# Latent input turned behind every second grouped tile, and a group norm made token tile by token tile

## What is computed

```python
def spatial_gating(z, v_norm, w_s, b_s):          # layer 0
    z = jax.nn.gelu(z)                            # z: (1, 1024, 512)
    u, vv = jnp.split(z, 2, axis=-1)
    u = u.reshape(b, s, B_GROUPS, B_GROUP_DIM)    # 4 groups of 64 columns
    vv = rmsnorm(vv.reshape(b, s, B_GROUPS, B_GROUP_DIM), v_norm)
    vv = vv.reshape(b, s // B_CHUNK, B_CHUNK, B_GROUPS, B_GROUP_DIM)   # chunks of 128 tokens
    mixed = jnp.einsum('gpq,bnqgc->bnpgc', w_s, vv) + b_s.T[None, None, :, :, None]
    return (u * mixed.reshape(b, s, B_GROUPS, B_GROUP_DIM)).reshape(b, s, B_WIDTH)

def mixer_odd(h, ...):                            # layer 1
    proj = h @ w_in
    ...
    cq = (rmsnorm(cq, cq_norm) @ w_cq_up).reshape(b, s, C_HEADS, C_NOPE + C_ROPE)
    kv = (rmsnorm(ckv, ckv_norm) @ w_ckv_up).reshape(b, s, C_HEADS, C_NOPE + C_V)
    ...
    dq = axial_rope(rmsnorm(dq.reshape(b, s, D_KV_HEADS, D_GROUP, HEAD_DIM), dq_norm), row, col)
    dk = axial_rope(rmsnorm(dk.reshape(b, s, D_KV_HEADS, HEAD_DIM), dk_norm), row, col)
    ...
```

## Time and profile before

| | |
|---|---|
| median of 3 runs | 4104.06 us (4103.8 to 4111.27) |
| profiled execution | 4103.9 us, span 4101.7 us |
| TensorE busy | 3662.3 us, 89% |
| VectorE busy | 2458.3 us, 60% |
| ScalarE busy | 1639.6 us, 40% |
| GpSimd busy | 329.3 us, 8% |
| mean granted clock of TensorE | 0.947 |

### The profile page before, as it was taken

How to read it: one execution, slowest core, us unless ns; L and a number is a source line. 1 busy time by engine, 2 the same in 40 slices (tenths; PEclk the granted TensorE clock), 3 DMA queues, 4 the chain that set the end, 5 groups by cost and what they waited for, 6 DMA issues and landing times. The chain is left out here.

```text
span 4101.7 us, 58119 instructions
## 1 busy us (share of the span) xinstructions
PE 3662.3 (89%) x23128; PEld 3009.7 (73%) x23128; DVE 2458.3 (60%) x3918; ACT 1639.6 (40%) x2308; POOL 329.3 (8%) x195
## 2 busy tenths in 40 slices
PE   6988999988999999999799999499788999994996
PEld 4767777877777888887599777377687877773774
DVE  3366671568765556566332663777664776637786
ACT  5223432158320000002221763367534766623775
POOL 0011111000000000000000000133200000001432
PEclk9989999999999999999899999799899999997998
DMA  5011223631431111112221324399723022043998
GB/s 196 16 50 37 75 75 121 240 117 36 157 136 74 55 41 60 42 41 82 93 86 57 132 86 154 143 372 371 268 86 121 28 88 81 23 149 125 371 366 295
DMA packets 194719, 527.57 MB, mean 129 GB/s; under 512 B 27512, under 2 KB 127656, under 8 KB 175424
## 3 DMA queue, kind: packets, MB, share of 16 engines
q1 hardware_dynamic: 178176, 467.21, 31.0%
q0 software_dynamic: 13200, 55.17, 4.6%
q10 hardware_dynamic: 3120, 2.10, 0.2%
HBM read 433.05 MB, written 91.37 MB: 128 GB/s over the span
## 5 line engine op out<-in xcount | busy, mean ns | idle before, releaser
L2556 ACT ACTIVATE mlp_relu<-mlp_z 128x512 f32<-128x512 f32 x64 | 38.3, 598 | 616.2 <-PE mlp_z L168 616.2
L3740 DVE TENSOR_TENSOR ring_r<-ring,oN_r 128x4096 fp32r<-128x4096 f32 x48 | 212.4, 4426 | 72.2 <-ACT oN_r L3646 72.2
L166 PE MATMUL scans_G<-ring_r 128*128 128x512 f32 x544 | 221.8, 408 | 32.3 <-ACT scans_stg L3106 18.3
L3740 DVE TENSOR_TENSOR ring_r<-ring,hT_r 128x4096 fp32r<-128x4096 f32 x48 | 212.5, 4427 | 51.3 <-ACT hT_r L3646 51.2
L3646 ACT ACTIVATE oN_r<-ring 128x4096 fp32r<-128x4096 f32 x48 | 174.0, 3629 | 81.0 <-DMA ring<-in_w_all 79.3
L166 PE MATMUL mlp_z<-oN_r,mlp_w_high_r 128*128 128x512 f32 x512 | 200.3, 391 | 5.6 <-DVE ring_r L2597 5.6
L167 PE MATMUL mlp_z<-hT_r,mlp_w_high_r 128*128 128x512 f32 x512 | 200.0, 391 | 0.0
L168 PE MATMUL mlp_z<-oN_r,ring_r 128*128 128x512 f32 x512 | 199.9, 390 | 0.0
L166 PE MATMUL mlp_y_ps<-mlp_w_high_r,ring_r 128*128 128x512 f32 x512 | 199.7, 390 | 0.0
L167 PE MATMUL mlp_y_ps<-ring_r 128*128 128x512 f32 x512 | 199.2, 389 | 0.0
L168 PE MATMUL mlp_y_ps<-mlp_w_high_r,ring_r 128*128 128x512 f32 x512 | 199.2, 389 | 0.0
(11 more groups left out here) (693 smaller groups left out, 10003.1 us busy)
## 6 DMA issues: line engine op xcount, KB each, us to landing
ring<-in_w_all SPq DMA_DIRECT2D x110, 2048.0 KB, 10.6
ring<-in_w_mlp SPq DMA_DIRECT2D x16, 2048.0 KB, 8.3
ring<-in_w_all SPq DMA_DIRECT2D x12, 1024.0 KB, 6.2
branch_gates<-scans_stg SPq DMA_DIRECT2D x48, 256.0 KB, 2.0
merge_raw<-branch_gates SPq DMA_DIRECT2D x16, 768.0 KB, 5.0
ring<-in_w_all POOLq DMA_DIRECT2D x8, 1024.0 KB, 6.0
diff_gemm_more<-in_w_all POOLq DMA_DIRECT2D x8, 1024.0 KB, 6.2
oN<-x_rows SPq DMA_DIRECT2D x16, 512.0 KB, 7.5
```

The costliest lines, as they stand in the source:

```text
L166: pe.matmul(out, lh, rh, start=start, stop=False)
L2556: act.activation(r[:, n % 2, :], Z[:, n % 4, :], ACT.Relu).then_inc(z_free, 1)
L3740: dve.tensor_tensor(buf_r[:, b, :], buf[:, b, :], w_high[n % RING].bitcast(F32), ALU.subtract)\
```

## The change

Two separate edits. In `odd_gemm_stage` the three latent groups are turned behind tiles 4, 6 and 8 instead of 4, 5 and 6, copied by ScalarE in the same turns, and their low parts are made in turns 5, 7 and 9 instead of 5, 6 and 7. In `spatial_stage` VectorE makes the squares, the sums and the product with the gain for each token tile as soon as its gelu is there; mean, root and reciprocal stay in one piece behind the last tile; the product with the reciprocal root is made group by group (four instructions of 128 x 512 instead of one of 128 x 2048), each of which lets TensorE start one group's mix.

```diff
--- before.py
+++ after.py
@@ -862,8 +862,8 @@
                     tile(NT + n, 1 + s_, t).then_inc(done, 1)
                 if n == 4:
                     pe.wait_ge(low_ready, NT)
-                if 4 <= n < 7:
-                    j = n - 4
+                if n in (4, 6, 8):
+                    j = (n - 4) // 2
                     if j:
                         pe.wait_ge(ct_used, j)
                     for t in range(NT):
@@ -947,9 +947,10 @@
                     act.activation(sq6, A[:, (NT + n) % 4, 0:NB * P], ACT.Square).then_inc(sq_in, 1)
                     act.wait_ge(root_in, n + 1)
                     act.activation(ss[:, n % 2, :], ss[:, n % 2, :], ACT.Sqrt).then_inc(root, 1)
-                if 4 <= n < 7:
-                    act.wait_ge(ct_done, n - 3)
-                    act.activation(c_high[:, n - 4, :], CT[:, :, :].rearrange("p a n -> p (a n)"), ACT.Copy).then_inc(ct_in, 1)
+                if n in (4, 6, 8):
+                    j = (n - 4) // 2
+                    act.wait_ge(ct_done, j + 1)
+                    act.activation(c_high[:, j, :], CT[:, :, :].rearrange("p a n -> p (a n)"), ACT.Copy).then_inc(ct_in, 1)
                 if n >= 1:
                     i = n - 1
                     act.wait_ge(xt_done, i + 1)
@@ -1066,10 +1067,11 @@
                 t5, v5 = (u.rearrange("p g (a b c) -> p g a b c", a=2, b=2) for u in (turned, v))
                 dve.tensor_tensor(t5[:, :, :, 0, :], t5[:, :, :, 0, :], v5[:, :, :, 1, :], ALU.subtract)
                 step(dve.tensor_tensor(t5[:, :, :, 1, :], t5[:, :, :, 1, :], v5[:, :, :, 0, :], ALU.add))
-                if 4 < n <= 7:
-                    dve.wait_ge(ct_in, n - 4)
-                    dve.tensor_tensor(c_low[:, n - 5, :], CT[:, :, :].rearrange("p a n -> p (a n)"),
-                                      c_high[:, n - 5, :].bitcast(F32), ALU.subtract).then_inc(ct_used, 1)
+                if n in (5, 7, 9):
+                    j = (n - 5) // 2
+                    dve.wait_ge(ct_in, j + 1)
+                    dve.tensor_tensor(c_low[:, j, :], CT[:, :, :].rearrange("p a n -> p (a n)"),
+                                      c_high[:, j, :].bitcast(F32), ALU.subtract).then_inc(ct_used, 1)
                 dve.wait_ge(root, n + 1)
                 step(dve.reciprocal(s2, s2))
                 dve.tensor_tensor(v, turned, s2.unsqueeze(2).to_broadcast([P, HEADS, 64]), ALU.mult).then_inc(x_ready, 1)
@@ -2713,8 +2715,8 @@
                     ins = three_passes(pe, Z[:, t % 4, :], [h[:, k, t * P:(t + 1) * P] for h in (h_high, h_low)],
                                        [v[:, k, :] for v in w], k == 0, k == KD - 1)
                 ins.then_inc(z_done, 1)
-            pe.wait_ge(v_ready, 1)
             for g in range(G):
+                pe.wait_ge(v_ready, g + 1)
                 if g >= 2:
                     pe.wait_ge(gated, g - 1)
                 v = z[:, :, W2 + g * C:W2 + (g + 1) * C]
@@ -2741,15 +2743,17 @@
                 dve.tensor_tensor(quarter(buf_r[:, slot, :], j), quarter(buf[:, slot, :], j),
                                   quarter(w_high, j).bitcast(F32), ALU.subtract).then_inc(w_split, 1)
             dve.wait_ge(par_in, 48)
-            dve.wait_ge(z_free, NT)
             v = z[:, :, W2:2 * W2].rearrange("p t (g c) -> p t g c", c=C)
-            group_squares(step, dve, v, sq[:, :, :].rearrange("p t (g c) -> p t g c", c=C), ss[:, :, :])
+            for t in range(NT):
+                dve.wait_ge(z_free, t + 1)
+                group_squares(step, dve, v[:, t, :, :], sq[:, t, :].rearrange("p (g c) -> p g c", c=C), ss[:, t, :])
+                dve.tensor_tensor(z[:, t, W2:2 * W2], z[:, t, W2:2 * W2], gn[:, :], ALU.mult)
             dve.tensor_scalar(ss[:, :, :], ss[:, :, :], 1.0 / C, EPS, ALU.mult, ALU.add).then_inc(root_in, 1)
             dve.wait_ge(root, 1)
             step(dve.reciprocal(ss[:, :, :], ss[:, :, :]))
-            step(dve.tensor_tensor(v, v, ss[:, :, :].unsqueeze(3).to_broadcast([P, NT, G, C]), ALU.mult))
-            dve.tensor_tensor(z[:, :, W2:2 * W2], z[:, :, W2:2 * W2],
-                              gn[:, :].unsqueeze(1).to_broadcast([P, NT, W2]), ALU.mult).then_inc(v_ready, 1)
+            for g in range(G):
+                dve.tensor_tensor(v[:, :, g, :], v[:, :, g, :], ss[:, :, g:g + 1].to_broadcast([P, NT, C]), ALU.mult)\
+                   .then_inc(v_ready, 1)
             for g in range(G):
                 dve.wait_ge(mixed, g + 1)
                 u = z[:, :, g * C:(g + 1) * C]
```

## The result

| | before | after |
|---|---|---|
| median | 4104.02 us (4098.1 to 4113.18, 6 runs) | 4085.55 us (4080.83 to 4088.72, 6 runs) |
| ratio to before | 1 | 0.995, 95% interval 0.9936 to 0.9963 |
| profiled execution | 4103.9 us, span 4101.7 | 4088.72 us, span 4086.6 |

The change makes the kernel 18.5 us faster by the medians, 15 to 26 us by the interval.

The account below looks back on a forecast made before the run. It took TensorE, busy for 89% of the span, to bound the kernel, with time won only where it stands still or runs at its lower clock. 13.2 + 7.7 = 20.9 us less gave 4083.0 us, range 4078.5 to 4091.

Parts of the forecast that it names:

- The thin margin: Grouped loop: TensorE reaches the second and third latent group about 0.5 us after VectorE's low part releases the PSUM tile.
- The 0.2 us in turn 10: Grouped loop: turn 10's transposes come late behind VectorE's turn with a low part, losing about 0.1 to 0.2 us.
- The split of the latent weights: Grouped loop, turn 10: nothing piles up ahead of this split; cost taken as nothing, bounds 0 and 1.22 us.
- a whole turn of VectorE behind a tile of TensorE: Grouped loop before the change: the claimed cost of a latent group, with TensorE idle 4.56 and 4.57 us.
- the clock's: Spatial stage's four mixes: the clock may rise one mix sooner, a gain of 0.4 us, bounds 0 to 0.9.
- The 0.5 us by which the first gating might have been late: Spatial stage: VectorE's first gating, queued behind the fourth product, ends up some 0.5 us past the first mix at worst.
- the loop's term: Grouped loop: 13.38 us less over four turns, less 0.2, gives a gain of 13.2 us, bounds 11 and 13.6.
- the spatial term: Spatial stage: first mix 7.3 us earlier plus 0.4 us of clock, a gain of 7.7 us, bounds 5.5 and 8.2.
- Rival 2: Grouped loop: the 0.5 us margin is used up by late turns, 2 us a group, 4087.0 us in all; chance 0.10.
- rival 3: Spatial gain hidden because the next stage waits for something other than the barrier; 13.2 us alone, 4090.7 us; chance 0.07.
- Rival 4: Waits behind the edits: clock after restarts falls otherwise, 3 us either way, 4080 to 4086; chance 0.78 together with rival 1.
- Rival 5: Grouped loop, tiles 6 to 15: clock falls to 1.2 GHz, 4.1 us a tile, 4115.8 us with eight; chance 0.02.

Follow-up runs that it names:

- experiment 3: Latent groups left behind tiles 4, 5 and 6, VectorE's low part moved ahead of its wait for the tile, spatial edit in; median 4081.1 us, ratio to before 0.9949.
- experiment 4: Changed kernel with the low part moved behind the product that TensorE waits for, at the end of VectorE's turn; single time 4080.27 us.
- `e6_fill`: Changed kernel with 15 unneeded matmuls of 512 columns in TensorE's wait ahead of the first mix; median 4084.3 us, ratio to before 0.9949.
- second set of runs: Each edit alone and both, beside the kernel before (4104.26 us): grouped 4090.72 us, spatial 4098.01 us, both 4084.43 us.
- `e11_before_again`: The kernel before, unchanged, run once more for its profile; single time 4108.61 us.
- experiment 6: Changed kernel with the second and third group of latent transposes made four times over, to the same place; single time 4089.07 us.

## Why the prediction was right

**The grouped loop.** Foretold 13.2 us; from turn 5's tile to the last transposes of the loop it was 78.17 before and 64.45 after, 13.7 us, and the edit alone moved the median by 13.5. Turns 5 to 8: foretold 22.62, measured 22.52, because a plain turn took 5.19 us and not 5.25. The thin margin, foretold as 0.58 and "about 0.5": 0.52 and 0.53. The 0.2 us in turn 10 is there (5.42), but it should not have been taken off: it vanishes in TensorE's wait for VectorE in turn 12 (experiment 3). The split of the latent weights got nothing on top, as taken. That missing the margin costs only the miss was a claim of one sentence; experiment 4 shows it for 0.3 us. What was incomplete is the reading behind it. The prediction called the cost "a whole turn of VectorE behind a tile of TensorE", as if it came with groups in a row; experiment 3 shows that the low part's place in the turn alone makes the wait. And the price of the clock is no fixed term: the 36.00 us were the short end of what the kernel before does, the same four turns took 37.90 us the next time.

**The spatial stage.** Foretold 7.3 us to the first mix; measured 7.40. The chain behind the last gelu ran as summed, with 0.20 us to spare for the root's table where 0.3 had been foretold. The term that was mis-sized is the clock's: I took 0.4 us of gain out of 0 to 0.9, because the lower clock had lasted 3.2 and 4.3 us after other restarts. The four mixes took 6.62 instead of 6.36 us: the term came out at -0.3 us, outside its own bounds, and the stage gave 7.1 and not 7.7. VectorE's waits for the mixes tell when each was done, in the kernel before and then in the changed one:

```profile
2024.93 0.75 DVE L2756 SCALAR_TENSOR_TENSOR oN<-spatial_mixed,spatial_bs,spatial_z 128x512 f32<-128x512 f32 x1 [0.95 <-PE spatial_mixed L2721]
2026.64 1.62 DVE L2756 SCALAR_TENSOR_TENSOR oN<-spatial_mixed,spatial_bs,spatial_z 128x512 f32<-128x512 f32 x2 [0.96 <-PE spatial_mixed L2721]
```

```profile
2020.24 0.75 DVE L2760 SCALAR_TENSOR_TENSOR oN<-spatial_mixed,spatial_bs,spatial_z 128x512 f32<-128x512 f32 x1 [0.95 <-PE spatial_mixed L2723]
2021.37 0.75 DVE L2760 SCALAR_TENSOR_TENSOR oN<-spatial_mixed,spatial_bs,spatial_z 128x512 f32<-128x512 f32 x1 [0.38 <-PE spatial_mixed L2723]
```

The third mix comes 1.71 us behind the second in both (2026.64 behind 2024.93; 2020.24 behind 2018.53), so three mixes were slow before as after, and the lower clock lasted over 5 us from the first. The trace of the kernel before held this, and two other waits were taken as the measure instead. Only the fourth mix differs: 1.13 us behind the third in the changed kernel, at most 0.9 before. Behind the waits of the other profiles the lower clock lasted up to 5.8 us (3045.78 to 3051.55 in the kernel with the spatial edit alone). The 0.5 us by which the first gating might have been late, queued behind four products, didn't come, because the first mix was slow: VectorE was there 0.36 us before it was done. With the mixes at the upper clock, in `e6_fill`, TensorE did wait for VectorE, 0.58 us.

**The sum.** The two stretches give 13.7 + 7.1 = 20.8 us, foretold 20.9. That this fits to 0.1 us is luck twice over: the loop's term was 0.5 too small and the spatial term 0.6 too large, and the profile of before was one with short stretches at the lower clock; against `e11_before_again`, where the loop took 80.06 us, the loop's edit gives some 15.5 us. The median gave 18.5, then 19.8 in the second set of runs. The difference from 20.8 lies within the interval; the untouched stages, which vary by 4 to 7 us each from one profile to the next, are enough to hide it. What is confirmed is the mechanism of either edit, in its stretch; that the forecast of the whole, 4083.0 us, is as near as it is, is in part chance.

**The rivals.** Rival 2 (the margin is used up) and rival 3 (the spatial gain hidden at the head of the next stage) didn't occur: that stage's first instruction moved by the whole 7.1 us. Rival 4 (the clock after restarts) is real: it is what makes the kernel before vary by 2 us in the grouped loop, and the change takes two such restarts out. Rival 5 (slower, the clock falls in unbroken work) fell with the changed kernel's own window (a clock of 1.00 over 23 us) and with experiment 6. Its price was also a little off: 24 x (0.375 - 0.207) is 4.0 us a tile and not 4.1, which changes nothing. One that I had not written down, that a DMA-bound stage gives a lead back, looked likely from the first two profiles of the changed kernel and went with the later ones.

## What to carry to other kernels

When an engine waits for a single buffer, look first at where in its reader's turn the release stands: an instruction whose inputs are ready before the turn begins belongs at its front, and spreading the writers out is the other cure. Price such a wait of TensorE as its idle time plus a stretch at half the clock (here 9.1 us idle and 3.5 to 5.5 us of clock for two waits); matmuls that nobody needs, put in the wait, show the two apart. And before a difference between two profiles is put down to a cause in a stage that no edit touched, take both profiles several times: here the second profile of the changed kernel repeated the difference, and only the third didn't.

## What the runs showed of the hardware

- TensorE's clock fell behind gaps of 4.56 us (all six, in three profiles) and 3.53 us (all eight profiles that have it). Behind the 4.56 us the stretch at 1.2 GHz after the restart was 3.2 to 5.8 us long, with no change in the code, and behind a gap of 4.97 us at the head of the stage after the spatial one 3.0 us in one kernel and 4.3 in another. The same two waits so cost 3.5 us of clock in one execution and 5.5 in the next.
- 35 transposes of float32 in a row (0.109 us each), begun at a granted clock of 1.00, left it there.
- ScalarE loaded the root's table (1.28 us) right behind the last gelu, 0.01 us after its end, and not when the root's input was there; so the load was off the path, though only by 0.20 us.
- In a stage where the DMA share is 0.99 the time varied from 334.6 to 339.1 us over 14 profiles.
